# One change at four places of a two-layer hybrid encoder kernel: who shifts, who copies, and how the memory keys are loaded

## The chip, the cores and the metric

The kernel runs on one core of a Trainium2 chip. The metric is the device time of one execution in microseconds; lower is better. TensorE multiplies matrices, VectorE, ScalarE and GpSimd work on rows of 128 partitions, SyncE issues most of the DMA transfers.

## The reference, cut to what matters

```python
for i in range(DEPTH):                       # DEPTH = 2: dilated attention, then latent attention
    mix = dilated_mixer(...) if i % 2 == 0 else mla_mixer(...)
    kv = mem @ w_kv[i]                       # mem (256, 1024), w_kv (1024, 512): keys and values
    mo = memory_attention(qm, mem, w_kv[i])
    y = concat([mix, mo]) @ w_out
    x = layer_norm(ALPHA * x + y, ln_mix_g[i], ln_mix_b[i])
    f = hierarchical_moe(x, ...)             # 32 experts, top-2 inside the top-1 group
    x = layer_norm(ALPHA * x + f, ln_ffn_g[i], ln_ffn_b[i])
# layer_norm(x) = (x - mean) * rsqrt(var + eps) * g + b, over 1024 elements, for 1024 tokens
```

## The kernel before, in words

There are 1024 tokens in eight tiles of 128 (tile 0 to 7). Every engine runs its own list of instructions, written out by hand; semaphores tie them together.

**Head.** TensorE begins with `mem_projection(0)`: keys (16 products, contraction in eight slices of 128) into bank 6, then values (16 products) into bank 7. SyncE's `mem_loads` issues the transposed memory tokens (1 MB), the key half of the weights (1 MB) and the value half (1 MB). After them come the loads of the first of three head groups: query weights, the first half of x transposed, its second half, key and value weights. TensorE's `group_projection(0)` waits for query weights and the first half of x. ScalarE copies the keys out (`mem_keys`), VectorE the values. The same `mem_projection` and `mem_loads` come again for layer 1, at the end of the experts of layer 0.

**Layer norms.** There are four of them, i = 0 to 3: i = 0 and 2 in the output projections, i = 1 after the experts of layer 0, i = 3 after the experts of layer 1. For each tile VectorE adds up the tile (`combine`: L1910 and L1913 in layer 0, L1925 in layer 1), takes its statistics (L1675, L1678), ScalarE takes the root (L1355), VectorE computes 1/std (L1682) and -mean/std (L1683) in `tile_rstd`, one tile later in its order, and ScalarE normalises the tile (L1357). GpSimd's `norm_scale` multiplies the tile by g (L718) and adds b (L720), tiles 0 to 6; VectorE does both for tile 7 (`last_scale`, L1691 and L1693). In i = 1 the tile is then transposed by TensorE (L1000), copied by ScalarE (L1362) and VectorE (L1698), and projected. In i = 3 SyncE stores tile by tile, in order (`wait_tokens`, L685), and the kernel ends with the last store.

**Experts and overflow.** Each of the 32 experts takes up to 96 token rows. Rows above that go to overflow blocks, a loop after the experts whose count is read from memory. In this data it runs once, in layer 1. One round: TensorE transposes and multiplies, ScalarE applies silu (L1392), VectorE gates, TensorE multiplies by the down weights, VectorE copies the results out of the banks (four copies 32x256, L1836, and two copies 64x512, L1839), and GpSimd scatters them to DRAM (L803). In the ordinary expert loop ScalarE (L1407, L1408) and VectorE share these copies half and half. After the overflow SyncE loads all expert results (L656) and TensorE sums them with gates (`expert_sums`).

Lines shown as L825 are the helper of all ordinary products.

Of the kernel before, what the change touches and what calls it, by code (L numbers as in the profile page):

```python
# [22 lines left out]
ALU = mybir.AluOpType  # L23
# [3 lines left out]
P = 128  # L27
# [41 lines left out]
def build(nc, io):  # L69
    with ExitStack() as ctx:  # L70
# [56 lines left out]
        def ring_at(kb, *shape):  # L127
# [65 lines left out]
        mem_in = sem("mem_in")  # L193
        mem_v_in = sem("mem_value_weights_in")
# [53 lines left out]
        x_last = sem("x_last_ready")  # L248
        last_gmul = sem("last_gmul_done")
# [55 lines left out]
               ("w_in", "slots", "idx", "xs", "pe_steps", "silu", "dve_steps", "out")}  # L305
# [52 lines left out]

        def wait_tokens(eng, i, t):

            if t < TT - 1:
                eng.wait_ge(x_ready, i * (TT - 1) + t + 1)
            else:
                eng.wait_ge(x_last, i + 1)
# [94 lines left out]
        def _(sp):  # L459

            def mem_loads(l):
                w = io["mem_w_kv"][l].rearrange("(k p) n -> p k n", p=P)
                sp.dma_start(mem_t[l], io["mem_t"].rearrange("(k p) n -> p k n", p=P)).then_inc(mem_in, 16)
                sp.dma_start(mem_w[l][:, :, 0:GW], w[:, :, 0:GW]).then_inc(mem_in, 16)
# [225 lines left out]
        def _(pool):  # L690
# [20 lines left out]
            def norm_scale(i, store_to=None):  # L711

                pool.wait_ge(gb_in, 32 * (i + 1))
                for t in range(TT):
                    n = i * (TT - 1) + t + 1
                    if t < TT - 1:
                        pool.wait_ge(norm_done, i * TT + t + 1)
                        nc.gpsimd.tensor_tensor(X[:, t], X[:, t], ln_gb[:, 0], ALU.mult).then_inc(gmul_done, 1)  # L718
                        pool.wait_ge(gmul_done, n)
                        nc.gpsimd.tensor_tensor(X[:, t], X[:, t], ln_gb[:, 1], ALU.add).then_inc(x_ready, 1)  # L720
# [4 lines left out]
            def experts(l):  # L725
# [73 lines left out]
                with pool.If(n_over > 0):  # L799
                    with pool.Fori(0, n_over) as j:  # L800
                        pool.wait_ge(o["dve_steps"], 4 * j + 4)
                        fence(pool)
# [20 lines left out]
        def _(pe):  # L823
# [3 lines left out]
            def mem_projection(l):  # L827

                pe.wait_ge(mem_in, 32 * (l + 1))
                for j in range(2):  # L830
                    for k in range(KT):
                        mm(ps[:, 6, j * MEM:(j + 1) * MEM], mem_w[l][:, k, j * P:(j + 1) * P], mem_t[l][:, k], k == 0, k == KT - 1)
# [27 lines left out]
            def group_projection(g):  # L860
# [11 lines left out]
                pe.wait_ge(wv_in[b], 16 * uses)  # L872
                for t in range(9 if g == 0 else 8):
# [188 lines left out]
            def experts(l):  # L1062
# [57 lines left out]
                with pe.If(n_over > 0):  # L1120
                    with pe.Fori(0, n_over) as j:
# [9 lines left out]
                        pe.wait_ge(o["dve_steps"], 4 * j + 4)  # L1131
                        fence(pe)
# [152 lines left out]
        def _(act):  # L1285
# [10 lines left out]
            def mem_keys(l):  # L1296
                act.wait_ge(mem_proj, l + 1)
                nc.scalar.copy(km_t[:], ps[:, 6].rearrange("p (a b) -> p a b", a=2)).then_inc(mem_kv_act, 1)
# [95 lines left out]
            def experts(l):  # L1394
# [23 lines left out]
                o = ov[l]  # L1418
                act.wait_ge(over_done, l + 1)
                n_over = act.value_load(over_i[0:1, NOVER:NOVER + 1], min_val=0, max_val=NOVER)  # L1420
                with act.If(n_over > 0):
                    with act.Fori(0, n_over) as j:
                        act.wait_ge(o["pe_steps"], 4 * j + 2)
                        silu().then_inc(o["silu"], 1)
                with act.Else():
                    act.nop()
# [107 lines left out]
        def _(dve):  # L1534
# [145 lines left out]
            def tile_rstd(i, t):  # L1680
                dve.wait_ge(sd_done, i * TT + t + 1)
                ln_link(nc.vector.reciprocal(rstd[:, t, 0:1], std[:, t:t + 1]))  # L1682
                nc.vector.scalar_tensor_tensor(out=rstd[:, t, 1:2], in0=mean_var[:, t, 0:1], scalar=-1.0, in1=rstd[:, t, 0:1],  # L1683
# [452 lines left out]
```

## Time and profile before

| what | us |
|---|---|
| runs of the kernel | 2440.29, 2444.55, 2451.59 |
| their median | 2444.55 |
| profiled execution, its own time | 2438.25 |
| profiled execution, its span | 2436.1 |

| engine | busy us | share of the span |
|---|---|---|
| TensorE (matmul) | 2222.6 | 91% |
| VectorE | 841.7 | 35% |
| ScalarE | 468.2 | 19% |
| GpSimd | 343.0 | 14% |

The times in the rows below are microseconds from the start of the span, and durations; means of one instruction are in ns. PE is TensorE's matmul, PEld its weight load, DVE VectorE, ACT ScalarE, POOL GpSimd, SPq SyncE's queue. In a timeline row the bracket tells how long the engine sat idle before the instruction and which work released it. A granted clock of 1.00 is 2.4 GHz, 0.50 is 1.2 GHz.

### The profile page before, as it was taken

How to read it: one execution, taken by the hardware profiler on the slowest of the kernel's cores; microseconds unless marked ns; L12 is line 12 of the kernel's file. 1: busy time of each engine (PE TensorE's matmuls, PEld its weight loads, DVE VectorE, ACT ScalarE, POOL GpSimd, SP SyncE). 2: the span in 40 equal slices, each digit the busy share in tenths (PEclk: the TensorE clock that was granted, in tenths of full speed). 3: DMA queues.
4: the chain of work that ended last, by engine and by line, in shares of the span. 5: the costliest groups of instructions: out<-in, count | busy, mean ns of one | idle time of the engine just before them, and what ended most of it. 6: DMA issues, size and time to landing. Idle time of an engine off the chain costs nothing. (4 is left out here: it accounts for less than half of the span.)

```text
span 2436.1 us, 37961 instructions
## 1 busy us (share of the span) xinstructions
PE 2222.6 (91%) x15351; PEld 1184.0 (49%) x15351; DVE 841.7 (35%) x1791; ACT 468.2 (19%) x943; POOL 343.0 (14%) x401
## 2 busy tenths in 40 slices
PE   8999998886999999998797999989689999999964
PEld 4665757553444444444443556665444444444422
DVE  2133324634121212122825767642422212121216
ACT  0030304221010101011333444431201101010011
POOL 0000000141111111131600000003211111111305
PEclk9999998987999999999897999999689999999997
DMA  9022104344999999997310000010469999999945
GB/s 352 1 76 98 40 1 142 141 184 165 396 391 388 394 386 389 389 387 274 119 52 7 3 5 1 1 70 35 200 224 395 388 400 384 386 378 391 375 158 207
DMA packets 98871, 534.47 MB, mean 219 GB/s; under 512 B 23040, under 2 KB 46880, under 8 KB 73824
## 3 DMA queue, kind: packets, MB, share of 16 engines
q1 hardware_dynamic: 80672, 491.28, 51.8%
q0 software_dynamic: 18112, 41.99, 4.8%
q8 instruction: 60, 0.98, 0.2%
q14 instruction: 27, 0.22, 0.0%
HBM read 510.16 MB, written 41.45 MB: 226 GB/s over the span
## 5 line engine op out<-in xcount | busy, mean ns | idle before, releaser
L825 PE MATMUL banks<-ring,arena 128*32 128x256 f32 (+3 forms) x9952 | 1303.4, 461 | 38.5 <-DMA ring<-in_exp_w_gu 15.0
L825 PEld LDWEIGHTS banks<-ring,arena 128*32 128x32 f32 (+2 forms) x9952 | 536.4, 124 | 746.3 <-issue 608.7
L825 PE MATMUL banks<-ring 128*128 128x512 f32 (+2 forms) x976 | 372.2, 531 | 10.7 <-ACT ring L1468 7.1
L825 PEld LDWEIGHTS banks<-ring 128*128 128x128 f32 (+1 forms) x976 | 183.9, 194 | 156.6 <-issue 139.8
L1830 DVE TENSOR_TENSOR arena<-arena,banks 128x384 f32<-128x384 f32 x65 | 36.0, 554 | 609.7 <-ACT arena L1392 609.7
L761 POOL DMA_INDIRECT expert_out<-arena,scatter_idx x64 | 61.1, 955 | 824.4 <-DVE arena L1839 804.4
L1392 ACT ACTIVATE arena<-banks 128x384 f32<-128x384 f32 x65 | 31.9, 490 | 735.8 <-PE banks L825 735.8
L825 PE MATMUL banks<-arena 128*64 128x128 f32 (+5 forms) x1664 | 157.8, 303 | 16.7 <-DMA arena<-in_mem_w_kv 9.6
L825 PEld LDWEIGHTS banks<-arena 128*64 128x64 f32 (+3 forms) x1664 | 139.0, 169 | 50.2 <-issue 38.0
L718 POOL TENSOR_TENSOR arena<-arena,ln_gb 128x1024 f32<-128x1024 f32 x28 | 69.5, 2482 | 626.5 <-ACT arena L1357 626.5
L1836 DVE COPY arena<-banks 32x256 f32<-32x256 f32 x132 | 56.2, 425 | 280.1 <-PE banks L825 279.2
L825 PE MATMUL banks<-arena,ring 128*128 128x256 f32 (+3 forms) x288 | 101.0, 529 | 13.6 <-DVE ring L1977 11.7
L1407 ACT COPY arena<-banks 32x256 f32<-32x256 f32 x128 | 46.2, 361 | 313.7 <-PE banks L825 313.0
L1600 DVE CUSTOM_DVE_ANT_0 arena<-banks,arena 128x256 f32<-128x256 f32 (+1 forms) x160 | 54.1, 394 | 148.8 <-PE banks L825 145.5
L1989 DVE TENSOR_REDUCE max_and_sum<-banks 128x1 f32<-128x1024 f32 x64 | 77.5, 1212 | 38.6 <-PE banks L825 38.2
L1482 ACT ACTIVATE arena<-banks,neg_max 128x1024 f32<-128x1024 f32 x64 | 71.3, 1114 | 91.7 <-DVE neg_max L1991 90.5
L1031 PEld LDWEIGHTS banks<-ident,arena 96*128 96x128 f32 x520 | 47.5, 146 | 66.3 <-issue 63.4
L1357 ACT ACTIVATE arena<-arena,ln_rstd 128x1024 f32<-128x1024 f32 x32 | 39.7, 1240 | 191.2 <-DVE ln_rstd L1683 191.2
L1031 PE MATMUL banks<-ident,arena 96*128 96x96 f32 x520 | 59.7, 260 | 16.6 <-issue 8.5
L825 PEld LDWEIGHTS banks<-arena,ring 128*128 128x128 f32 (+2 forms) x288 | 48.6, 183 | 51.7 <-issue 47.0
L720 POOL TENSOR_TENSOR arena<-arena,ln_gb 128x1024 f32<-128x1024 f32 x28 | 71.1, 2539 | 2.2
L1826 DVE COPY arena<-banks 128x768 f32<-128x768 f32 x65 | 62.3, 958 | 24.9 <-PE banks L1031 17.5
(176 smaller groups left out, 1575.7 us busy)
## 6 DMA issues: line engine op xcount, KB each, us to landing
ring<-in_exp_w_gu SPq DMA_DIRECT2D x130, 2048.0 KB, 17.2
ring<-in_exp_w_down SPq DMA_DIRECT2D x65, 2048.0 KB, 21.8
ring<-in_x_t SPq DMA_DIRECT2D x6, 2304.0 KB, 16.4
moe_in<-arena POOLq DMA_DIRECT2D x16, 512.0 KB, 3.0
arena<-expert_out SPq DMA_DIRECT2D x16, 512.0 KB, 4.3
ring<-expert_out SPq DMA_DIRECT2D x16, 512.0 KB, 4.4
ring<-in_a_w_in SPq DMA_DIRECT2D x6, 1024.0 KB, 17.3
arena<-in_a_w_in SPq DMA_DIRECT2D x4, 1024.0 KB, 14.0
```

The lines of the kernel that those rows point to most:

```text
L718: nc.gpsimd.tensor_tensor(X[:, t], X[:, t], ln_gb[:, 0], ALU.mult).then_inc(gmul_done, 1)
L720: nc.gpsimd.tensor_tensor(X[:, t], X[:, t], ln_gb[:, 1], ALU.add).then_inc(x_ready, 1)
L761: pool.indirect_dma_start(y_d[l][:, :], bass.IndirectOffsetOnAxis(ap=s_idx[0:CAP, b:b + 1], axis=0), ys[0:CAP, b], None, bounds_check=2 * ...
L825: return nc.tensor.matmul(out, lhsT, rhs, start=start, stop=stop)
L1031: last = nc.tensor.transpose(ps[:, k // 4, (k % 4) * CAP:(k % 4 + 1) * CAP], xs[0:CAP, b, k * P:(k + 1) * P], ident[0:CAP, 0:CAP])
L1357: nc.scalar.activation(X[:, t], X[:, t], ACT.Identity, bias=rstd[:, t, 1:2], scale=rstd[:, t, 0:1]).then_inc(norm_done, 1)
L1407: nc.scalar.copy(ys[WIDE:CAP, b, g * 256:(g + 1) * 256], ps[NARROW * g:NARROW * g + NARROW, 7, 0:256])
L1482: nc.scalar.activation(prob[:, hd], ps[:, 2 * hd:2 * hd + 2].rearrange("p a b -> p (a b)"), ACT.Exp, bias=neg_max[:, hd, 0:1], scale=SCALE ...
L1600: last = nc.vector.tensor_tensor_reduce(out=prob[:, b, h * 256:h * 256 + w], in0=ps[:, 2 * b + h % 2, (h // 2) * 256:(h // 2) * 256 + w], ...
L1826: return V.tensor_copy(xs_t[b].rearrange("p (a c) n -> p a (c n)", a=2), ps[:, 0:2, 0:4 * CAP])
L1836: return V.tensor_copy(ys[WIDE:CAP, b, g * 256:(g + 1) * 256], ps[NARROW * g:NARROW * g + NARROW, 7, 0:256])
L1989: V.tensor_reduce(stat[:, hd, 0, 0:1], ps[:, 2 * hd:2 * hd + 2].rearrange("p a b -> p (a b)"), AX.X, ALU.max).then_inc(row_max, 1)
```

## The change

1. `mem_loads` loads the tokens and the key weights in two halves of the contraction, each half with a semaphore of its own. `mem_projection` does the products of the first half when it is there, then those of the second; its two 128-column halves of the keys lie in banks 5 and 6. TensorE waits for ScalarE's copy of the keys before it writes the value products of a group, which use bank 5.
2. In the last layer norm (i = 3) VectorE adds b for tiles 1, 3 and 5; GpSimd keeps all scales and the adds of tiles 0, 2, 4 and 6.
3. In the overflow round ScalarE copies half of the results, as in the expert loop.
4. In `tile_rstd` -mean/std is computed by an operation with one tensor input and a scalar per partition, in place of two tensor inputs and one scalar.

```diff
         def wait_tokens(eng, i, t):
-            if t < TT - 1:
+            if i == 3 and t in SHIFT_ON_DVE:          # SHIFT_ON_DVE = (1, 3, 5)
+                eng.wait_ge(x_shifted, SHIFT_ON_DVE.index(t) + 1)
+            elif i == 3 and t < TT - 1:
+                eng.wait_ge(x_ready, i * (TT - 1) + t + 1 - sum(o < t for o in SHIFT_ON_DVE))
+            elif t < TT - 1:
                 eng.wait_ge(x_ready, i * (TT - 1) + t + 1)
...
             def mem_loads(l):
-                sp.dma_start(mem_t[l], io["mem_t"].rearrange("(k p) n -> p k n", p=P)).then_inc(mem_in, 16)
-                sp.dma_start(mem_w[l][:, :, 0:GW], w[:, :, 0:GW]).then_inc(mem_in, 16)
+                for ks, landed in ((slice(0, KT // 2), mem_in), (slice(KT // 2, KT), mem_rest_in)):
+                    sp.dma_start(mem_t[l][:, ks], io["mem_t"].rearrange("(k p) n -> p k n", p=P)[:, ks]).then_inc(landed, 16)
+                    sp.dma_start(mem_w[l][:, ks, 0:GW], w[:, ks, 0:GW]).then_inc(landed, 16)
...
             def norm_scale(i, store_to=None):
-                        pool.wait_ge(gmul_done, n)
-                        nc.gpsimd.tensor_tensor(X[:, t], X[:, t], ln_gb[:, 1], ALU.add).then_inc(x_ready, 1)
+                        if not (i == 3 and t in SHIFT_ON_DVE):
+                            pool.wait_ge(gmul_done, n)
+                            nc.gpsimd.tensor_tensor(X[:, t], X[:, t], ln_gb[:, 1], ALU.add).then_inc(x_ready, 1)
...
                     with pool.Fori(0, n_over) as j:
                         pool.wait_ge(o["dve_steps"], 4 * j + 4)
+                        pool.wait_ge(o["y_act"], j + 1)
...
             def mem_projection(l):
-                pe.wait_ge(mem_in, 32 * (l + 1))
-                for j in range(2):
-                    for k in range(KT):
-                        mm(ps[:, 6, j * MEM:(j + 1) * MEM], mem_w[l][:, k, j * P:(j + 1) * P], mem_t[l][:, k], k == 0, k == KT - 1)
+                for half, landed in enumerate((mem_in, mem_rest_in)):
+                    pe.wait_ge(landed, 32 * (l + 1))
+                    for j in range(2):
+                        for k in range(4 * half, 4 * half + 4):
+                            mm(ps[:, 5 + j, 0:MEM], mem_w[l][:, k, j * P:(j + 1) * P], mem_t[l][:, k], k == 0, k == KT - 1)
...
             def group_projection(g):
                 pe.wait_ge(wv_in[b], 16 * uses)
+                pe.wait_ge(mem_kv_act, 1)
...
                         pe.wait_ge(o["dve_steps"], 4 * j + 4)
+                        pe.wait_ge(o["y_act"], j + 1)
...
             def mem_keys(l):
-                nc.scalar.copy(km_t[:], ps[:, 6].rearrange("p (a b) -> p a b", a=2)).then_inc(mem_kv_act, 1)
+                nc.scalar.copy(km_t[:], ps[:, 5:7, 0:MEM]).then_inc(mem_kv_act, 1)
...
                 o = ov[l]                                  # ScalarE, after its last expert
+                for b in range(2):
+                    act.wait_ge(ys_out[b], 16 * 16 * (l + 1))
...
                         silu().then_inc(o["silu"], 1)
+                        act.wait_ge(o["pe_steps"], 4 * j + 4)
+                        for g in range(2):
+                            nc.scalar.copy(ys[WIDE:CAP, 0, g * 256:(g + 1) * 256], ps[NARROW * g:NARROW * g + NARROW, 7, 0:256])
+                        nc.scalar.copy(ys[0:WIDE, 0, 0:HALF], ps[0:WIDE, 6]).then_inc(o["y_act"], 1)
...
             def tile_rstd(i, t):
-                nc.vector.scalar_tensor_tensor(out=rstd[:, t, 1:2], in0=mean_var[:, t, 0:1], scalar=-1.0, in1=rstd[:, t, 0:1],
-                                               op0=ALU.mult, op1=ALU.mult).then_inc(rs_done, 1)
+                nc.vector.tensor_scalar(rstd[:, t, 1:2], mean_var[:, t, 0:1], rstd[:, t, 0:1], -1.0, ALU.mult, ALU.mult).then_inc(rs_done, 1)
...
                         dve.wait_ge(o["pe_steps"], 4 * j + 4)
-                        for g in range(4):
+                        for g in range(2, 4):
                             narrow_out(0, g)
-                        wide_out(0, 0)
                         wide_out(0, 1).then_inc(o["dve_steps"], 1)
...
                     if t == TT:
                         last_scale(i)
+                    if l == 1 and t - 3 in SHIFT_ON_DVE:
+                        dve.wait_ge(gmul_done, i * (TT - 1) + t - 2)
+                        nc.vector.tensor_tensor(X[:, t - 3], X[:, t - 3], ln_gb[:, 1], ALU.add).then_inc(x_shifted, 1)
```

## Rows read from the trace of the kernel before

**Rows 1.** Stretches: start:end, length, PE, PEld, DVE, ACT, POOL, clock, DMA, GB/s.
```profile
600.00:1150.00 550.00, 538.69 (x4823) 240.70 (x4816) 109.84 (x188) 56.80 (x127) 85.14 (x134) 1.00 0.96 380
1777.00:1794.00 17.00, 15.40 (x116) 6.74 (x115) 10.55 (x21) 0.49 (x1) 2.58 (x5) 0.79 0.17 41
```
**Rows 2.** SyncE's timeline at the start; DMA issues with KB and us to landing.
```profile
0.74 0.44 SPq L463 DMA_DIRECT2D arena<-in_mem_t  x1
...
6.62 2.92 SPq L480 DMA_DIRECT2D ring<-in_x_t  x1
...
arena<-in_mem_t SPq DMA_DIRECT2D x1, 1024.0 KB, 5.7
...
ring<-in_x_t SPq DMA_DIRECT2D x1, 2304.0 KB, 14.9
```
**Rows 3.** TensorE's timeline: memory products of layer 0, and the gap in layer 1.
```profile
9.59 15.46 PE L825 MATMUL banks<-arena 128*128 128x256 f32 x64 [9.59 <-DMA arena<-in_mem_w_kv]
24.89 86.18 PE L825 MATMUL banks<-ring 128*128 128x512 f32 x272
...
1166.68 1.94 PE L1000 MATMUL banks<-ident,arena 128*128 128x128 f32 x8 [15.19 <-issue]
```
**Rows 4.** Timeline of one tile of the layer norm between the layers.
```profile
1182.87 3.22 POOL L720 TENSOR_TENSOR arena<-arena,ln_gb 128x1024 f32<-128x1024 f32 x1
...
1185.50 0.61 DVE L1683 SCALAR_TENSOR_TENSOR ln_rstd<-ln_mean_var,ln_rstd 128x1 f32<-128x1 f32 x1
...
1187.29 0.56 ACT L1362 COPY arena<-banks 128x512 f32<-128x512 f32 x1
...
1187.95 1.07 PE L1000 MATMUL banks<-ident,arena 128*128 128x128 f32 x8 [0.54 <-issue]
...
1195.28 1.06 PE L1000 MATMUL banks<-ident,arena 128*128 128x128 f32 x8 [0.68 <-issue]
```
**Rows 5.** Timeline: copies of the overflow round, and ScalarE's in an ordinary expert.
```profile
2367.47 1.72 DVE L1836 COPY arena<-banks 32x256 f32<-32x256 f32 x4 [5.62 <-PE banks L825]
2369.21 1.39 DVE L1839 COPY arena<-banks 64x512 f32<-64x512 f32 x2
...
1827.44 0.73 ACT L1407 COPY arena<-banks 32x256 f32<-32x256 f32 x2 [4.80 <-PE banks L825]
```
**Rows 6.** Timeline of the last layer norm, VectorE and GpSimd.
```profile
2392.29 0.16 DVE L1683 SCALAR_TENSOR_TENSOR ln_rstd<-ln_mean_var,ln_rstd 128x1 f32<-128x1 f32 x1
...
2392.88 1.22 DVE L1925 TENSOR_TENSOR arena<-arena,banks 128x1024 f32<-128x1024 f32 x1 [0.43 <-PE banks L825]
...
2396.31 1.22 DVE L1925 TENSOR_TENSOR arena<-arena,banks 128x1024 f32<-128x1024 f32 x1
...
2398.63 2.36 POOL L718 TENSOR_TENSOR arena<-arena,ln_gb 128x1024 f32<-128x1024 f32 x1
...
2399.02 0.11 DVE L1682 RECIPROCAL ln_rstd<-ln_std 128x1 f32<-128x1 f32 x1
...
2399.16 1.84 DVE L1683 SCALAR_TENSOR_TENSOR ln_rstd<-ln_mean_var,ln_rstd 128x1 f32<-128x1 f32 x1
...
2424.73 3.20 POOL L720 TENSOR_TENSOR arena<-arena,ln_gb 128x1024 f32<-128x1024 f32 x1
2425.77 3.24 DVE L1693 TENSOR_TENSOR arena<-arena,ln_gb 128x1024 f32<-128x1024 f32 x1
```
**Rows 7.** The last store, issued at 2429.04: us to landing; and a stretch (columns of rows 1).
```profile
DMA to landing us min/median/max: 2.8/2.8/2.8
...
2429.00:2430.00 1.00, 0.00 (x0) 0.00 (x0) 0.01 (x1) 0.00 (x0) 0.00 (x0) 0.50 1.01 406
```
**Rows 8.** Timeline in the routing of layer 0: GpSimd's memset, and VectorE's operations beside it.
```profile
547.21 1.80 POOL L728 MEMSET arena<- 128x2048 f32 x1 [9.71 <-PE banks L825]
...
548.53 0.19 DVE L1745 TENSOR_TENSOR arena<-logits,arena 128x32 f32<-128x32 f32 x1
548.64 0.41 DVE L1747 TENSOR_SCALAR arena<-arena 128x32 f32<-128x32 f32 x1
```

More of the change, by code:

```diff
@@ L193, in build @@
         mem_in = sem("mem_in")
+        mem_rest_in = sem("mem_rest_in")
         mem_v_in = sem("mem_value_weights_in")
@@ L248, in build @@
         x_last = sem("x_last_ready")
+        x_shifted = sem("x_shifted_by_dve")
         last_gmul = sem("last_gmul_done")
@@ L304, in build @@
         ov = [{n: sem(f"ov{l}_{n}") for n in
-               ("w_in", "slots", "idx", "xs", "pe_steps", "silu", "dve_steps", "out")}
+               ("w_in", "slots", "idx", "xs", "pe_steps", "silu", "dve_steps", "y_act", "out")}
               for l in range(DEPTH)]
@@ L357, in straight @@
                     step((0, u), u + 1 < TT, 0 <= u < TT, u >= 1)
+        SHIFT_ON_DVE = (1, 3, 5)
         def wait_tokens(eng, i, t):
-            if t < TT - 1:
+            if i == 3 and t in SHIFT_ON_DVE:
[3 more added lines that the diff above has]
+            elif t < TT - 1:
                 eng.wait_ge(x_ready, i * (TT - 1) + t + 1)
```

## Prediction

> **What bounds the kernel now.** I read the busy shares by stage first, then the timeline at each of the four places that the diff touches, since an average says nothing of a few microseconds. In the expert phases TensorE is busy 98% of the time at a granted clock of 1.00 [rows 1], and none of the four places lies in them: each is a stage with a limit of its own.
>
> *The head.* SyncE issues the memory tokens, the key weights behind them and, later, the first x. Tokens and x land at 0.74 + 5.7 = 6.4 and 6.62 + 14.9 = 21.5 us [rows 2]. TensorE starts its 32 memory products at 9.59, released by the key weights, and goes over to the group projection at 24.89 with no gap [rows 3]. So the first wait is a load and the next 15.3 us are TensorE's own.
>
> *The layer norm between the layers.* [Rows 4] show one token tile; the next one's transposes come 7.33 us later. The tiny L1683 (one element per partition) takes 0.61 us and ends just after GpSimd's L720 (1182.87 + 3.22 = 1186.09). ScalarE's norm waits for it, ScalarE's copy L1362 comes behind the norm, and TensorE's next transposes start when that copy is done (1187.95), after an idle 0.54 us.
>
> *The overflow block.* It runs once, in layer 1. VectorE copies four narrow and two wide results alone, 1.72 + 1.39 us from 2367.47 to 2370.60 [rows 5], and scatter, reloads and expert sums queue behind it.
>
> *The tail.* [Rows 6]: undisturbed L1683 takes 0.16 us; here it takes 1.84 and ends with GpSimd's op (2398.63 + 2.36 = 2400.99). Seven tiles times scale and shift keep GpSimd full, 14 ops of some 2.35 us. The last one is stretched to 3.20 us by VectorE's scale of tile 7, and VectorE's shift (L1693) waits in turn until 2427.93 and ends at 2429.01. Two-tensor operations of the two engines exclude each other. The stage is one chain through that shared access.
>
> **The change, part by part.**
>
> *Keys in halves.* The first half of tokens and of key weights is as many bytes as the tokens alone, so it lands near 6.4 instead of 9.4 us; two more issues at about 0.44 us each [rows 2] stand ahead of loads that wait for bandwidth, so I cost them at 0.1 us of the start. TensorE begins at about 6.5. Half of the key products takes some 5 us (15.46 us for 32, the first ones slower), to 11.5, when the second half has landed: it is there when the whole was, 9.5. No new wait. All end at 24.89 - 3.1 = 21.8, and the first x landed at 21.5: covered by 0.3 us. **3.0 us**; with x landing 0.5 us late it is 2.7. The bounds are 0 (TensorE waits for x or for the second half) and 3.1. The added wait for the key copy stands ahead of the value products, 50 us after that copy: nothing. Group projections and attention follow TensorE, and the loads behind them are triggered by it, so the gain is carried on. In layer 1 the same split gains nothing: TensorE idles 15.19 us behind the memory products there [rows 3], waiting for the first normalised tile. The five issues there stand ahead of one load only.
>
> *The small operation*, between the layers. If it no longer waits, L1683 takes the 0.16 us of its undisturbed form [rows 6], ScalarE's copy comes 0.45 us earlier, and TensorE's gap of 0.54 us shrinks by that. VectorE asks for the shared access for the next tile's sum 0.4 us earlier, just as it comes free at 1186.09, so the tile's cycle shrinks from 7.33 to about 6.9 us; TensorE's own work is 7.33 - 0.68 = 6.65. Five tiles have such a gap (two of them in rows 4): 5 x 0.4 = **2.0 us**. Bounds 0 and 5 x 0.54 = 2.7. In the two output projections the operation already takes 0.16 us in the median: 0.
>
> *Overflow copies.* VectorE keeps two of four narrow copies and one of two wide ones, 0.86 + 0.70 = 1.56 us in place of 3.13. ScalarE's half runs beside it, as in every expert, where its two narrow copies take 0.73 us [rows 5] and its wide one is of VectorE's order. The function table that ScalarE loaded ahead of the tail is now loaded after these copies, 1.28 us, ended 15 us before its first use. ScalarE, GpSimd and TensorE wait for semaphores that are set by then. **1.5 us**, bounds 1.2 and 1.6.
>
> *Three shifts on VectorE*, with a small operation that does not wait. TensorE hands over a tile every 3.43 us (2392.88, 2396.31 [rows 6]) and VectorE's work on one is 3.0 us (2392.88 to 2395.88). From GpSimd's scale of tile 1, which ends at 2401.0: scale 2 to 2403.4; VectorE shift 1, asked for at 2399.75 + 3.0 = 2402.8, to 2404.5 (1.08 us each, the part of L1693 after 2427.93); GpSimd shift 2 to 2406.8, scale 3 to 2409.2, scale 4 to 2411.6; VectorE's tile 6 work ends at 2410.7 and shift 3 runs to 2412.7; GpSimd shift 4 to 2415.0, scale 5 to 2417.4, scale 6 to 2419.9; VectorE scale 7 to 2421.0, GpSimd shift 6 to 2423.3, VectorE shift 7 to 2424.4. Only then, since the code puts it behind the scale and shift of tile 7, shift 5 to 2425.5. What comes late is the store: SyncE waits in order of tiles, so tiles 5, 6 and 7 are issued together from 2425.5. Now the last store lands 2.8 us after 2429.04, at 2431.8; the last two are 1.05 MB at 406 GB/s [rows 7], 2.6 us, so 1.3 us of latency from the issue at 2427.95. Three are 3.9 us, after the same latency from 2425.5: 2430.7. So of 3.5 us on the engines the end sees **1.2 us**; bounds -2.9 (below) and 3.5.
>
> **Sum:** 3.0 + 2.0 + 1.5 + 1.2 = 7.7 us. The profiled execution took 2438.25 us for a span of 2436.1, so 2430.5; the median of the runs shown is 6.3 us above it, and the forecast for the median is 2444.55 - 7.7 = **2436.9 us**.
>
> **The rivals.**
>
> *The small operation still waits.* [Rows 8] show a VectorE operation with one tensor input, 128x32, of 0.41 us that ends just when GpSimd's memset ends (547.21 + 1.80 = 549.01); tensor operations of two inputs beside it took 0.19 us and did not wait. So one input is no safe pass. Then the 2.0 us between the layers are gone. In the tail tile 2's norm comes at 2401.0 as before, scale 2 ends at 2404.8, shift 1 at 2405.9, and on: shift 2 2408.2, scale 3 2410.6, scale 4 2414.3, shift 3 2415.4, shift 4 2417.8, scale 5 2420.2, scale 6 2423.9, shift 6 2426.3, VectorE 2427.4, 2428.5 and shift 5 2429.6; stores land at 2429.6 + 1.3 + 3.9 = 2434.8, 3 us later than now. Sum 3.0 + 1.5 - 2.9 = 1.6 us: 2442.9. For it: the 0.41 us. Against: the reciprocal beside L1683, of one element and one input, takes 0.11 us with GpSimd running [rows 6].
> [...]
>
> *The clock* (the slower side). The first expert of layer 1 ran in a stretch with a mean granted clock of 0.79, most of the expert phase at 1.00 [rows 1], where an expert takes about 550 / 32 = 17 us. If work shifted by 3 us leaves the clock at 1.2 GHz for one more expert, its 17 us become 34: 2436.9 + 17 = 2453.9, slower than before. It decides from a low stretch that costs 7.7 us, 15.4 us long at half speed. Nothing in the diff asks for it; the runs shown, 11.3 us apart, show that such amounts occur. The same in our favour gives about 2428.
>
> *The head's gain does not come*, because the first x lands later behind more issues, or the halves land together: 7.7 - 3.0, 2439.9.
>
> **How the numbers follow.** Forecast 0.52, small operation still waiting 0.26, head without gain 0.08, clock against 0.06, clock in favour 0.08. The range is 2429 to 2446: it takes in the first three cases with their bounds and some microseconds of scatter, and leaves out the clock cases. A measurement of this kernel can tell about 0.5%, 12.2 us, from no change. 7.7 us is 0.3%: faster by more takes the clock's help, 0.12; slower by more two mishaps, 0.03; within it 0.85.
>
> **What would show it.** TensorE's first product near 6.5 us and the group projection near 21.9. L1683's successor at 0.16 us everywhere; 0.6 and 1.8 us would be the first rival. TensorE's gaps in the norm between the layers below 0.3 us. Overflow copies over in 1.6 us. GpSimd with 11 operations in the tail, over 4.6 us sooner (2423.3 for 2427.9, the gains before it aside), three stores issued together. Wrong would be: a gap ahead of the group projection, shifts of tiles 1 and 3 that hold up the next tile's sum by more than a microsecond, or a time outside 2429 to 2446.

## The result, and the profile after

| | before | after |
|---|---|---|
| median of 8 runs, us | 2441.34 (2440.00 to 2451.59) | 2428.40 (2424.64 to 2433.50) |
| profiled execution, its own time | 2438.25 | 2429.48 |
| its span | 2436.1 | 2427.6 |
| ratio of the runs, with its 95% interval | | 0.9946 [0.9933, 0.9959] |

The change is 0.54% faster, 12.9 us in the medians and 8.5 us in the two spans. The forecast was 2436.9 us, a gain of 7.7. Of the 8.5 us between it and the measured 2428.4, 3.2 are the reference's (three runs of before had a median of 2444.55, eight have 2441.34) and 5.2 are a gain larger than forecast.

In the rows below the line numbers are those of the changed kernel: TensorE's helper is L836, its transposes L1013, the small operation L1703, GpSimd's scale L727 and add L730, VectorE's scale and add of tile 7 L1710 and L1712, its new adds L1957, the last store L694.

**The head.** TensorE's timeline (start, duration, engine, line, operation, count, and in the bracket the idle time and its releaser); it answers to [rows 3]:

```profile
6.80 15.63 PE L836 MATMUL banks<-arena 128*128 128x256 f32 x64 [6.80 <-DMA arena<-in_mem_w_kv]
22.26 8.32 PE L836 MATMUL banks<-ring 128*128 128x512 f32 x19
```

TensorE starts 2.79 us earlier and reaches the group projection 2.63 us earlier (22.26 for 24.89), with no gap in the products and none ahead of the projection. Neither the second half nor the first x is waited for; x lands at 6.77 + 14.9 = 21.7, 0.6 us ahead of the projection.

**Between the layers.** All eight uses of the small operation in this stage, before and then after (duration in ns: min/median/max), and two tiles' transposes after; they answer to [rows 4]:

```profile
L1683 DVE SCALAR_TENSOR_TENSOR ln_rstd<-ln_mean_var,ln_rstd x8: 159/600/607, 1158.2 to 1204.0; 128x1 f32<-128x1 f32 x8
```
```profile
L1703 DVE TENSOR_SCALAR ln_rstd<-ln_mean_var,ln_rstd x8: 214/214/215, 1156.9 to 1201.0; 128x1 f32<-128x1 f32 x8
```
```profile
1185.27 2.65 POOL L727 TENSOR_TENSOR arena<-arena,ln_gb 128x1024 f32<-128x1024 f32 x1 [0.98 <-ACT arena L1371]
...
1185.77 1.06 PE L1013 MATMUL banks<-ident,arena 128*128 128x128 f32 x8 [0.28 <-issue]
...
1192.70 1.06 PE L1013 MATMUL banks<-ident,arena 128*128 128x128 f32 x8 [0.28 <-issue]
...
1207.01 1.06 PE L1013 MATMUL banks<-ident,arena 128*128 128x128 f32 x8 [0.73 <-DVE arena L1717]
```

The operation takes 0.214 us every time, whether GpSimd runs beside it or not. TensorE's gap is 0.28 us where it was 0.54 and 0.68, and a tile takes 6.93 us (1192.70 - 1185.77) where it took 7.33. GpSimd now starves: it waits 0.98 us for ScalarE's norm. The last gap of this stage stays: ahead of one tile's transposes TensorE waits 0.73 us for VectorE's copy, as it did in the kernel before:

```profile
1209.98 1.06 PE L1000 MATMUL banks<-ident,arena 128*128 128x128 f32 x8 [0.73 <-DVE arena L1698]
```

**Overflow.** Timeline of the copies, which answers to [rows 5]:

```profile
2365.23 0.73 ACT L1443 COPY arena<-banks 32x256 f32<-32x256 f32 x2 [7.40 <-PE banks L836]
2365.23 0.86 DVE L1855 COPY arena<-banks 32x256 f32<-32x256 f32 x2 [5.62 <-PE banks L836]
2365.97 0.58 ACT L1444 COPY arena<-banks 64x512 f32<-64x512 f32 x1
2366.11 0.69 DVE L1858 COPY arena<-banks 64x512 f32<-64x512 f32 x1
2366.57 1.28 ACT L1369 ACT_TABLE_LOAD   x1
```

VectorE is done in 1.57 us (2365.23 to 2366.80) instead of 3.13, ScalarE beside it in 1.32. The table load stands where it was expected and nobody waits for it.

**The tail.** VectorE's first add of a tile's sums, before and then after, and after from the first of the new adds on; the last answers to [rows 6, 7]:

```profile
2386.08 1.22 DVE L1925 TENSOR_TENSOR arena<-arena,banks 128x1024 f32<-128x1024 f32 x1 [15.49 <-PE banks L825]
```
```profile
2383.10 1.22 DVE L1943 TENSOR_TENSOR arena<-arena,banks 128x1024 f32<-128x1024 f32 x1 [16.30 <-PE banks L836]
...
2399.74 1.72 DVE L1957 TENSOR_TENSOR arena<-arena,ln_gb 128x1024 f32<-128x1024 f32 x1
...
2407.32 2.08 DVE L1957 TENSOR_TENSOR arena<-arena,ln_gb 128x1024 f32<-128x1024 f32 x1
...
2415.65 1.63 DVE L1710 TENSOR_TENSOR arena<-arena,ln_gb 128x1024 f32<-128x1024 f32 x1 [1.38 <-ACT arena L1371]
2416.28 3.20 POOL L730 TENSOR_TENSOR arena<-arena,ln_gb 128x1024 f32<-128x1024 f32 x1
2417.32 3.25 DVE L1712 TENSOR_TENSOR arena<-arena,ln_gb 128x1024 f32<-128x1024 f32 x1
2420.49 1.21 DVE L1957 TENSOR_TENSOR arena<-arena,ln_gb 128x1024 f32<-128x1024 f32 x1
2421.73 1.64 SPq L694 DMA_DIRECT2D out_x<-arena  x3
```

The three stores go out together, as foreseen. To compare executions I count from VectorE's first add of tile sums, 2386.08 before and 2383.10 after, to the end of the span, and call this **the tail**: 50.0 us before, 44.5 after. The tail term was forecast at 1.2 us and is 5.5.

Most of the expectations below count from the first product of the expert sums instead, 2379.92 before and 2376.43 after: 56.2 and 51.2 us. That count takes in TensorE's sums for the first tile, and these depend on the granted clock: in the first 15 us of the expert sums it was 0.84 before, 0.81 after and 0.88 in a second trace of the changed kernel (y1), and VectorE's first add came 6.2, 6.7 and 5.6 us after the first product. From the first add on, executions of one kernel agree within 0.03 us.

Where the rest is, the last rows tell. First SyncE's waits at its end (total us, count, longest), before and then after; behind them, before, the traffic after the last store was issued (columns of rows 1):

```profile
SPq L70 <- PEq L70: 4.0, 1, 4.0
SPq L70 <- DMA out_x<-arena: 2.5, 1, 2.5
```
```profile
SPq L70 <- DMA out_x<-arena: 3.6, 1, 3.6
SPq L70 <- PEq L70: 0.5, 1, 0.5
```
```profile
2431.00:2432.00 1.00, 0.00 (x0) 0.00 (x0) 0.00 (x0) 0.00 (x0) 0.00 (x0) 0.50 0.36 139
...
2433.00:2436.00 3.00, 0.00 (x0) 0.00 (x0) 0.00 (x0) 0.00 (x0) 0.00 (x0) 0.50 0.00 0
```

Before, the last store had landed at 2429.04 + 2.8 = 2431.8 and the span still ran for 4.3 us, in which nothing moves and no engine is busy. SyncE sits those 4.0 us at the program's last line, behind the wait for its stores. After, the wait for the stores is longer (three at once) and the one behind it is 0.5 us. The name PEq is no help: TensorE had long been done. GpSimd's last operation is its add, which ends at 2424.73 + 3.20 = 2427.93 before and at 2419.48 after, and the span ends 8.2 us behind it in both (8.16 by the unrounded trace).

What lies between is recorded. At the program's last line each engine has an instruction DRAIN. GpSimd's and SyncE's before, then GpSimd's after (view of L70: duration in ns, start):

```profile
L70 POOLq DRAIN  x1: 11172/11172/11172, 2424.7 to 2424.7; - x1
...
L70 SPq DRAIN  x1: 13/13/13, 2432.0 to 2432.0; - x1
```
```profile
L70 POOLq DRAIN  x1: 11176/11176/11176, 2416.2 to 2416.2; - x1
```

GpSimd's ends at 2424.7 + 11.2 = 2435.9 before, 7.9 us after its add and 3.8 us after SyncE's; then the engines exchange semaphores and the span ends 0.2 us later. The description ahead of the prediction, by which the kernel ends with the last store, is not borne out. Why GpSimd's DRAIN takes 7.9 us beyond its last operation, no run here shows.

### The profile page after: what moved, and what is told of

It is laid out like the page before. It is cut to its first block and busy times, and to the rows that moved or that the text cites. A ratio compares the mean times of both kernels' runs of the same rounds, so it can differ in the third digit from the quotient of the medians.

```text
span 2427.6 us, 37971 instructions
## 1 busy us (share of the span) xinstructions
PE 2220.2 (91%) x15351; PEld 1185.3 (49%) x15351; DVE 833.2 (34%) x1791; ACT 469.4 (19%) x946; POOL 338.9 (14%) x398
## 5 line engine op out<-in xcount | busy, mean ns | idle before, releaser
L836 PE MATMUL banks<-ring,arena 128*32 128x256 f32 (+3 forms) x9952 | 1302.0, 461 | 38.5 <-DMA ring<-in_exp_w_gu 16.1
L836 PEld LDWEIGHTS banks<-ring,arena 128*32 128x32 f32 (+2 forms) x9952 | 536.6, 124 | 744.6 <-issue 606.8
L836 PE MATMUL banks<-ring 128*128 128x512 f32 (+2 forms) x976 | 369.3, 528 | 11.9 <-ACT ring L1488 7.1
L836 PEld LDWEIGHTS banks<-ring 128*128 128x128 f32 (+1 forms) x976 | 182.4, 192 | 156.9 <-issue 140.4
L836 PE MATMUL banks<-arena 128*64 128x128 f32 (+5 forms) x1664 | 159.0, 305 | 14.0 <-DMA arena<-in_mem_w_kv 6.8
L836 PEld LDWEIGHTS banks<-arena 128*64 128x64 f32 (+3 forms) x1664 | 140.1, 170 | 47.2 <-issue 34.9
L727 POOL TENSOR_TENSOR arena<-arena,ln_gb 128x1024 f32<-128x1024 f32 x28 | 69.4, 2481 | 627.0 <-ACT arena L1371 627.0
L836 PE MATMUL banks<-arena,ring 128*128 128x256 f32 (+3 forms) x288 | 99.4, 523 | 13.8 <-DVE ring L1998 11.7
L836 PEld LDWEIGHTS banks<-arena,ring 128*128 128x128 f32 (+2 forms) x288 | 48.4, 182 | 50.6 <-issue 45.7
L758 POOL DMA_INDIRECT arena<-moe_in,gather_idx x64 | 62.9, 983 | 55.5 <-POOL gather_idx L755 55.5
```

Of the source, the lines that this page charges most:

```text
L758: pool.indirect_dma_start(xs[0:CAP, b], None, x1_d[l][:, :], bass.IndirectOffsetOnAxis(ap=g_idx[0:CAP, b:b + 1], axis=0), bounds_check=S - ...
L836: return nc.tensor.matmul(out, lhsT, rhs, start=start, stop=stop)
```

## The experiments

Two theories of the tail: the span ends with the last store's landing (as the prediction had it), or it ends some 8.2 us after GpSimd's last operation, unless the stores land later. And for each part of the change: what is it worth alone, and with the others? All times of the table are from one profiled execution each. The second column counts from the first product of the expert sums to the end of the span; the tail, the end of GpSimd's last operation and the issue and landing of the last store count from VectorE's first add.

| kernel | from the first product | tail | GpSimd's end | last store issued | last store landed | ratio of the runs |
|---|---|---|---|---|---|---|
| before | 56.2 | 50.0 | 41.9 | 43.0 | 45.8 | |
| the change | 51.2 | 44.5 | 36.4 | 39.5 | 43.9 | 0.9946 [0.9933, 0.9959] |
| the change again (x0) | 51.1 | 44.5 | 36.4 | 39.5 | 43.9 | 0.9945 [0.9928, 0.9963] |
| the change again (y1) | 50.1 | 44.5 | 36.4 | 39.5 | 43.9 | 0.9953 [0.9936, 0.9970] |
| small operation alone (x1) | 57.6 | 51.0 | 42.9 | 43.3 | 46.9 | 0.9992 [0.9978, 1.0005] |
| shifts alone (x2) | 55.4 | 48.9 | 39.8 | 44.2 | 48.5 | 1.0001 [0.9988, 1.0013] |
| overflow copies alone (x3) | 55.2 | 50.0 | 41.9 | 43.0 | 45.8 | 1.0002 [0.9991, 1.0013] |
| halves alone (x4) | 56.0 | 50.0 | 41.9 | 43.0 | 45.8 | 1.0003 [0.9991, 1.0016] |
| halves alone, again (x11) | 56.2 | 50.0 | 41.9 | 43.0 | 45.8 | 0.9998 [0.9987, 1.0010] |
| before, GpSimd touched last (x5) | 57.7 | 51.3 | 43.1 | 43.0 | 45.8 | 1.0014 [0.9999, 1.0029] |
| change with the two-input operation (x7) | 55.7 | 48.9 | 39.8 | 44.2 | 48.6 | 0.9983 [0.9972, 0.9993] |
| change, tile 6 shifted too (x6) | 47.8 | 42.2 | 33.1 | 38.1 | 41.9 | 0.9936 [0.9914, 0.9957] |
| the same again (y3) | 49.1 | 42.3 | 33.1 | 38.1 | 41.9 | 0.9951 [0.9934, 0.9968] |
| change, shifts placed earlier (x9) | 50.1 | 44.5 | 36.4 | 38.8 | 41.4 | 0.9966 [0.9953, 0.9978] |
| tile 6 too, and earlier (x8) | 48.6 | 42.1 | 33.1 | 38.1 | 41.7 | 0.9946 [0.9929, 0.9964] |
| change without halves (x10) | 51.3 | 44.5 | 36.4 | 39.5 | 43.9 | 0.9964 [0.9951, 0.9976] |
| the same again (y2) | 51.2 | 44.5 | 36.4 | 39.5 | 43.9 | 0.9952 [0.9934, 0.9970] |

**The change again (x0), no edit.**

> The changed kernel once more, for a second trace of it and of its scatter. If the clock's steps are what moved TensorE by up to 4 us between stages, they fall in other places here, while the tail (from VectorE's first tile sum to the end of the span) takes the same 44.5 us, within 0.2. If the tail varies by more, part of the tail's gain is scatter too.

From VectorE's first tile sum to the end 44.5 us, as expected; group projection at 22.1, the small operation 0.214 us in the median: all repeated.

**GpSimd touched last (x5).** GpSimd waits for VectorE's last add and then sets 128 words that nobody reads:

```diff
+            pool.wait_ge(x_last, 4)
+            nc.gpsimd.memset(eps[:, 1:2], RMS_EPS).then_inc(zeroed, 1)
```

> The kernel before with one more GpSimd operation, a memset of one element per partition that waits for tile 7 to be finished (at 2429.0 in the trace of before), beside the last store. Theory D counted from the start of GpSimd's last operation: the span ends 11.2 us after 2429.1, 4.3 us later than before. Theory D counted from its end (7.9 us): the memset takes 0.1 us, so the span ends near 2437.1, 1.2 us later. Theory S (4.3 us after the last store lands): unchanged, within 0.3 us.

The timeline's last lines, SyncE's waits and GpSimd's DRAIN of this kernel:

```profile
2428.16 1.41 SPq L685 DMA_DIRECT2D out_x<-arena  x2
2429.28 0.10 POOL L821 MEMSET eps<- 128x1 f32 x1 [1.14 <-DVE arena L1695]
```
```profile
SPq L70 <- PEq L70: 5.2, 1, 5.2
SPq L70 <- DMA out_x<-arena: 2.5, 1, 2.5
```
```profile
L70 POOLq DRAIN  x1: 8052/8052/8052, 2429.3 to 2429.3; - x1
```

Stores as before, and an operation of 0.10 us on GpSimd, ended at 2429.38, moves the end to 2437.5, 8.2 us behind it; GpSimd's DRAIN ends at 2437.3, again 7.9 us behind the operation. SyncE's last wait grows from 4.0 to 5.2 us, by as much as GpSimd's end moved from its add (2424.93 + 3.20 = 2428.13, now 2429.38: 1.25). The end is tied to GpSimd. The table says the same of all: wherever the last store is issued at most 3.1 us after GpSimd's end, tail minus GpSimd's end is 8.2 us (8.16 or 8.17 before rounding; before, the change and its repeats, x1, x3, x4, x5, x9, x10, x11, y2), whether the last landing is 0.7 or 5.5 us ahead of the end. Where the stores are later (x2, x6, x7, x8, y3) it is 9.0 to 9.2, and the tail ends 0.4 us behind the last landing (0.39 or 0.40 before rounding); in x6 SyncE's DRAIN is at 2422.8, GpSimd's is over at 2411.4 + 10.5 = 2421.9. So in all 17 executions the span ends with the later of two, GpSimd's last operation plus 8.2 us and the last landing plus 0.4.

**The shifts alone (x2).** Of the change's diff only `SHIFT_ON_DVE`, the waits in `wait_tokens`, the skipped add in `norm_scale` and the add in `combine`.

> The kernel before with the three shifts on VectorE alone; the small operation keeps its two tensor inputs. Theory D (the span ends when GpSimd's queue drains, 11.2 us after its last operation starts, or with the last store if that is later): VectorE's waits for GpSimd stay, so GpSimd's last operation starts only some 0.6 us earlier and the stores land 2.6 us later, which brings both ends together: the span is 0 to 1 us shorter. Theory S (the span ends 4.3 us after the last store lands, as my prediction had it): 2.6 us longer. Both within 0.2%, so the trace decides: which comes last, and by how much.

Two of GpSimd's operations in its timeline:

```profile
2402.84 2.35 POOL L725 TENSOR_TENSOR arena<-arena,ln_gb 128x1024 f32<-128x1024 f32 x1
...
2406.56 2.35 POOL L725 TENSOR_TENSOR arena<-arena,ln_gb 128x1024 f32<-128x1024 f32 x1 [1.37 <-ACT arena L1365]
```

GpSimd has three operations of 2.35 us less, 7 us, and its end moves by 2.1: it now sits idle for ScalarE's norm, 4.3 us in all, since the norm waits for VectorE's small operation and that for GpSimd. The last store lands 2.7 us later than before, yet the tail is 1.1 us shorter: the end didn't follow the stores here either. The gain of 1.1 us isn't seen in the runs.

**The small operation alone (x1).**

```diff
-                nc.vector.scalar_tensor_tensor(out=rstd[:, t, 1:2], in0=mean_var[:, t, 0:1], scalar=-1.0, in1=rstd[:, t, 0:1],
-                                               op0=ALU.mult, op1=ALU.mult).then_inc(rs_done, 1)
+                nc.vector.tensor_scalar(rstd[:, t, 1:2], mean_var[:, t, 0:1], rstd[:, t, 0:1], -1.0, ALU.mult, ALU.mult).then_inc(rs_done, 1)
```

> The kernel before with the small operation alone. Between the layers TensorE's gaps shrink to 0.28 us: 1.6 us gained, as in the trace of the changed kernel. In the tail GpSimd still has 14 operations and nothing is taken off it. Theory D: its last operation starts no earlier, perhaps 1 us later, because VectorE no longer keeps out of step with it: sum -1.6 to 0 us. Rival (the small operation alone gives the tail's gain): -1.6 - 4 = -5.6 us.

From the first transposes of this stage (TensorE's L1000) to the first product behind the last ones 49.1 us (1171.26 to 1220.36) instead of 50.7 (1166.68 to 1217.35): 1.6 gained between the layers. In the tail 1.0 lost: VectorE is done early with tile 7, GpSimd has all 14 operations and is the last, as its rows show:

```profile
2420.15 3.32 POOL L718 TENSOR_TENSOR arena<-arena,ln_gb 128x1024 f32<-128x1024 f32 x1
2423.55 3.20 POOL L720 TENSOR_TENSOR arena<-arena,ln_gb 128x1024 f32<-128x1024 f32 x1
2426.72 2.33 POOL L718 TENSOR_TENSOR arena<-arena,ln_gb 128x1024 f32<-128x1024 f32 x1
2429.13 2.34 POOL L720 TENSOR_TENSOR arena<-arena,ln_gb 128x1024 f32<-128x1024 f32 x1
```

**The change with the old small operation (x7).** The reverse of the diff above, in the changed kernel.

> The changed kernel with the small operation undone (two tensor inputs again). Between the layers the gaps of TensorE go back from 0.28 to 0.54 to 0.7 us: 1.6 us lost. In the tail VectorE waits for GpSimd in every tile again. Theory D: GpSimd's last operation starts about 4 us later than in the changed kernel, stores land 4 us later: together 5.5 to 6 us slower than the changed kernel, 2.5 to 3.5 us faster than before. Rival: the small operation has little part in it, and the tail's gain comes from the shifts alone: 1.6 us slower than the changed kernel.

Tail 48.9 us, as with the shifts alone, and 50.7 us between the layers. VectorE's small operation, up to 2.02 us in the tail, is what binds the two engines to each other. So in the tail the shifts alone give 1.1 us, the small operation alone costs 1.0, and both give 5.5: the two are one measure. Against the change the old operation costs 4.4 + 1.6 = 6.0 us in the traces and 6.25 in the medians (2436.15 to 2429.9 of the change beside it), a little more than expected, and the rival's 1.6 is excluded.

**Tile 6 shifted too (x6, y3), and the order of the adds (x9, x8).**

```diff
-        SHIFT_ON_DVE = (1, 3, 5)
+        SHIFT_ON_DVE = (1, 3, 5, 6)
```

> The changed kernel with VectorE adding b for tile 6 as well, so GpSimd's last operation is the scale of tile 6. Theory D: GpSimd's last operation starts 2.4 us earlier and ends 3.4 us earlier, the stores land nearly 5 us earlier, and the span is shorter than that of the changed kernel by 2.4 us (counted from the start) or 3.2 us (from the end). Theory S: shorter by 4.9 us. Against the kernel before: a ratio of about 0.993 to 0.9945.

```profile
2409.26 4.64 POOL L727 TENSOR_TENSOR arena<-arena,ln_gb 128x1024 f32<-128x1024 f32 x2
...
2413.34 1.64 DVE L1710 TENSOR_TENSOR arena<-arena,ln_gb 128x1024 f32<-128x1024 f32 x1 [1.38 <-ACT arena L1371]
2415.01 1.23 DVE L1712 TENSOR_TENSOR arena<-arena,ln_gb 128x1024 f32<-128x1024 f32 x1
2416.16 2.36 DVE L1957 TENSOR_TENSOR arena<-arena,ln_gb 128x1024 f32<-128x1024 f32 x2
```

GpSimd ends at 2413.9, VectorE's add of tile 7 takes 1.23 us instead of 3.25 with GpSimd out of the way, and the tail is 42.2 us: 2.3 shorter (by the count of the expectation 47.8, 3.4 shorter, but 1.1 of that is the clock in the first tile's sums). Now the stores end last, 4.1 us after the last issue at 2418.92. The next two runs move VectorE's adds ahead of tile 7's, without and with tile 6:

```diff
-                    if t == TT:
-                        last_scale(i)
                     if l == 1 and t - 3 in SHIFT_ON_DVE:
                         dve.wait_ge(gmul_done, i * (TT - 1) + t - 2)
                         nc.vector.tensor_tensor(X[:, t - 3], X[:, t - 3], ln_gb[:, 1], ALU.add).then_inc(x_shifted, 1)
+                    if t == TT:
+                        last_scale(i)
```

> The change with one thing altered: VectorE's shift of tile 5 stands ahead of the scale and shift of tile 7. Theory that GpSimd's last operation sets the end: it still has the add of tile 6 last, at the same time, so the tail stays at 51.2 us (50.7 to 51.7) although the stores are issued earlier; median as the change, within 1 us. Rival, that the stores set the end, as the prediction had it: tile 5 stored 2.3 us earlier, tail 49 us.

> The change with VectorE adding b for tiles 1, 3, 5 and 6 too, and with the shift of a tile placed ahead of the scale and shift of tile 7 in VectorE's order, so that tile 5 is stored earlier. Theory that the span ends with the later of two, GpSimd's last operation plus 7.9 us and the last store's landing: with shift 6 on VectorE alone the end was the stores' (last issue at 2418.92, tail of 47.8 us from the first expert sum). Moved ahead, shift 5 lets its store go some 2.3 us earlier, so the three last stores no longer queue: tail 46.5 us (46.0 to 47.2), GpSimd's last operation as there, and a median about 1.3 us below that of shift 6 alone. Rival, that the order costs as much as it gives because the scale of tile 7 comes later: tail 47.8 or more.

x9: the last store lands 2.5 us earlier (41.4 for 43.9), GpSimd's end is unmoved (36.4), and so is the tail (44.5). That is the expectation, seen once the count starts at VectorE's first add; from the first product the tail reads 50.1, because the granted clock in the first 15 us of the sums was 0.88 and not 0.81. SyncE's waits say the same (2.3 us for the stores, then 2.9):

```profile
SPq L70 <- PEq L70: 2.9, 1, 2.9
SPq L70 <- DMA out_x<-arena: 2.3, 1, 2.3
```

The runs of x9 were no faster than the change's (2432.26), and y1, the change unaltered, has the same 50.1 at the same clock. x8 has a tail of 42.1, only 0.15 us less than x6 and y3: the rival was right, tile 7 pays for the earlier tile 5.

**Overflow copies alone (x3).** The hunks of `y_act` and ScalarE's three copies.

> The kernel before with the overflow copies shared alone. From the end of the down products to the scatter's issue 1.5 us less, and nothing else moves: -1.5 us in the span, 0.06%, below what the timing can tell; the trace has to show it. Rival: ScalarE's table load or the added wait holds up the tail: 0.

From the gating to the scatter 9.9 us (2359.57 to 2369.47) instead of 11.4 (2360.10 to 2371.47): 1.5 gained in the trace. The runs don't resolve it.

**The halves alone (x4, x11), and the change without them (x10, y2).** The hunks of `mem_loads`, `mem_projection`, `mem_keys` and the wait in `group_projection`, added to the kernel before, and taken from the changed one.

> The kernel before with the memory keys in halves alone. TensorE starts at 6.8 us and the group projection at 22.3: -2.6 us. Theory carried on: the whole of it is left at the start of the layer norm between the layers, and the span is 2.6 us shorter, plus or minus the clock's steps of up to 4 us seen between the two traces. Rival: the later stages give it back, because the experts are bound by loads that do not start earlier: 1.2 to 1.4 us left after the experts of layer 0, as in the trace of the changed kernel.

> The halves alone, once more, beside the other kernels of this call. In the trace the gain of 3.2 us was there at the start of layer 1's experts and gone in the span, where TensorE had spent 107 us at the lower clock in the latent attention stage instead of 85 to 99. Theory that this is scatter of the clock: starts at group projection 22.4, ratio 0.9987 (0.9980 to 1.0000). Rival, that the halves alone put the kernel into a worse course of the clock each time: ratio 1.000 to 1.002 and over 100 us at the lower clock in that stage again.

> The change without the halves of the memory loads; the other three parts stay. If the head's gain of 3.2 us is carried through the whole kernel: group projection at 25.7 instead of 22.3, span and median 3.2 us longer than the change, ratio to before about 0.9960. Rival, that the gain is lost on the way (the halves alone gave no difference in the timed rounds, 1.0003 [0.9991, 1.0016]): ratio as the change, 0.9946 to 0.995.

TensorE's timeline at the start, of x4 and of x10:

```profile
6.41 16.14 PE L827 MATMUL banks<-arena 128*128 128x256 f32 x64 [6.41 <-DMA arena<-in_mem_w_kv]
22.39 3.17 PE L827 MATMUL banks<-ring 128*128 128x512 f32 x7
```
```profile
9.58 17.04 PE L834 MATMUL banks<-arena 128*128 128x256 f32 x64 [9.58 <-DMA arena<-in_mem_w_kv]
26.46 1.88 PE L834 MATMUL banks<-ring 128*128 128x512 f32 x4
```

The traces are clear for the first half of the kernel. Over the nine executions with halves (x8 left out: its first attention took some 9 us longer, at a mean granted clock of 0.94 where the change had 0.97) and the seven without, the mean start of the group projection is 22.3 against 25.7 us, of the first expert's transposes 569.7 against 573.2, and of the first transposes between the layers 1164.8 against 1168.5, the last difference uncertain by about 1.6 us. Further on they don't show it. The expert sums start at 2377.1 against 2380.2, but the kernels with halves have the overflow copies and the new small operation more often than those without, which accounts for 0.9 of these 3.1 us; the 2.2 that are left are uncertain by about 3. The runs see less. Halves alone: 1.0003 with an interval from 0.9991, which leaves out 3 us (0.9988), and 0.9998 with one from 0.9987, which just takes it in; together a mean of 2441.0 us in 23 runs, where the kernel before beside them has 2441.2 in 46. Of the two readings of x11 the rival, a worse course of the clock each time, fell: from its first product to the experts' first transposes the latent attention took 551.7 us in x4, the longest of all, and 543.0 in x11, the shortest. Three kernels were then timed side by side:

> The change itself again, beside the two kernels of this call. Ratio to before 0.9945 (0.993 to 0.996), tail 51.1 us from the first expert sum to the end of the span.

> The change without the halves of the memory loads, again, in one call with the change. Theory that the head's gain reaches the end: the median is 3 us (1.5 to 4.5) above the change's of this call, as it was across calls (0.9964 to 0.9946). Rival, that the gain is lost in the stages behind, as the two runs of the halves alone suggest (1.0003 and 0.9998): within 1 us of the change's.

> The change with VectorE adding b for tile 6 too (in the change's own order), again, in one call with the change. Theory that the end follows GpSimd's last operation until the stores take over: tail 47.8 us, 3.3 us shorter than the change, median 3 us (1.5 to 4.5) below it. Rival, that the profile's end is not what the time sees: within 1 us of the change's.

Medians 2428.75, 2429.59 and 2429.32. The change's ratio came as expected (0.9953), its count from the first product did not (50.1 for 51.1, the clock in the first tile's sums). Both other medians lie within 1 us of the change's, where their rivals had them, but six to nine runs that spread over 7 to 15 us exclude neither side. Over all runs, the mean is 2429.4 for the change (23 runs), 2430.3 without halves (12) and 2426.8 with tile 6 shifted too (12), each uncertain by about 1.5 to 3 us. The halves' 3 us are in the traces up to the layer norm between the layers; in the time they are not shown, and the runs of the halves alone speak against the whole of them. The best kernel measured is x6/y3, by about 2.6 us in the mean, not certain beyond its scatter.

**What scatters.** The latent attention is the same code in all these kernels. The same stretch before and in x7 (start:end, length, PE, PEld, DVE, ACT, POOL, clock, DMA, GB/s):

```profile
1219.00:1784.00 565.00, 504.00 (x2780) 303.94 (x2780) 302.90 (x616) 197.76 (x359) 44.13 (x31) 0.90 0.11 42
```
```profile
1219.00:1780.00 561.00, 496.99 (x2781) 301.58 (x2781) 303.36 (x617) 197.82 (x359) 44.16 (x31) 0.92 0.11 43
```

The same products take 504 us at a mean granted clock of 0.90 and 497 at 0.92. Over all executions that stage, from its first product (1228.52 before) to the first transposes of layer 1's experts (1775.84), ranges from 543.0 to 551.7 us. A gain of 3 us upstream is smaller than that.

## Why the prediction was right, and where it failed

**What failed is one step, the tail's last sentence**: "So of 3.5 us on the engines the end sees 1.2 us"; the term measured 5.5. It took the landing of the last store for the end. Its own figures show the gap: the store lands at 2431.8, the span ends at 2436.1, and 4.3 us were left unexplained. They belong to GpSimd: the program isn't over until 8.2 us after GpSimd's last operation (x5, and eleven more rows of the table). With that, the step's own arithmetic gives GpSimd 4.6 us sooner (2423.3 for 2427.9, which the text lists among the signs and doesn't count), and a tail of 50.0 - 4.6 = 45.4; measured 44.5.

The schedule itself held within 0.9 us. Counted from VectorE's first add of tile sums (2386.08 before, 2383.10 after):

| | predicted | measured |
|---|---|---|
| VectorE's add of tile 1 ends | 18.4 | 18.4 |
| VectorE's add of tile 3 ends | 26.6 | 26.3 |
| GpSimd's last operation ends | 37.2 | 36.4 |
| VectorE's add of tile 7 ends | 38.3 | 37.5 |
| VectorE's add of tile 5 ends | 39.4 | 38.6 |
| last store lands | 44.6 | 43.9 (3.6 us after its issue ended at 2423.37) |

The stores' gain was 1.9 us for 1.2: landing at 45.8 before and 43.9 after. One sign that the prediction had named as wrong did come: VectorE's shifts hold up its next tile sum, that of tile 5 by 1.2 us and that of tile 7 by 2.3 (18.3 and 26.2 us after the first add, for 17.1 and 24.0 in x1, which has no shifts). It cost the tail next to nothing, since GpSimd's 11 operations still ran with only 0.1 us of idle time between them.

**The other terms.** The head: forecast 3.0, 2.6 in the profiled pair, 3.3 over the 16 executions; its cover (x landing 0.3 us ahead) held. That the gain is carried on to the end is not shown. Between the layers: 2.0 forecast, 1.6 measured (50.7 to 49.1 in every kernel with the new operation). The prediction counted five gaps that shrink; the trace before has four (0.54, 0.68, 0.67 and 0.73 us), and the last stays, because TensorE waits for VectorE's copy there; and the operation takes 0.21 and not 0.16 us. Overflow: 1.5 and 1.5 (scatter after gating 11.37, now 9.89). Sum with the tail's 5.5: 3.3 + 1.6 + 1.5 + 5.5 = 11.9 us, against 12.9, 11.7 and 11.4 in the medians of three sets of runs. In the profiled pair the terms make 2.6 + 1.6 + 1.5 + 5.5 = 11.2, and the spans differ by 8.5: 1.2 us of the head's lead are gone at the first transposes between the layers (1166.68 before, 1165.27 after), 0.5 go in the first tile's sums, and the other 1.0 between them.

**The rivals.** *The small operation still waits*: fell, 0.214 us in all places. The Trainium skill's rule (SBUF — State Buffer, "Who interferes with whom", with the condition of VectorE: DVE Perf Modes, "Mode 2×_2P") has a VectorE operation with one tensor input contend with GpSimd only in a mode that needs an outermost non-unit dimension that is even, or odd and equal in source and destination. One element per partition has no non-unit dimension, so by the rule the new operation doesn't contend, and the trace agrees with its 0.214 us. The rival's computed order of events is that of x7, though, where the old operation stays: last store landed 48.7 us after the first add by the rival (2434.8 - 2386.1), 48.6 in x7. *The clock*: its price was right in kind, as the latent attention's 543 to 552 us show, but in the profiled pair that stage took 547.3 us in both. *The head's gain doesn't come*: it came in every trace at the group projection; whether the time has it is open.

**The range** was short by 0.6 us at its lower end for two reasons of like size, the tail (4.3 us) and the three runs' median (3.2). Each alone would have stayed inside. The second is luck of the three runs and no mechanism. The chance for "faster" by over 0.5%, 0.12, followed from the same step: with the tail at 5.5 us the sum would have been 12.0, next to the 12.2 us that make 0.5%.

## What to carry to other kernels

Before the end of a kernel is priced, account for the whole stretch from the last transfer's landing to the end of the span: if microseconds are left over, look which engine's last operation stands a fixed time ahead of the end in another execution too. Here that was GpSimd, so its last operation, and not the last store, was to be made early. Count a stage from a point behind the stretch that the clock moves: from the first product, repeats of one kernel differed by 1.1 us, from VectorE's first add by 0.01. And of two edits to one coupled stage, price the pair: here one was worth 1.1 us alone, the other -1.0, and both together 5.5.

## What the hardware showed

- The program's end lay 8.2 us after the end of GpSimd's last operation in twelve of the seventeen executions, even if that operation was a 0.10 us memset (x5). In the other five it lay 0.4 us after the last store's landing. GpSimd's DRAIN at the program's last line ended 7.9 us after its last operation in all seventeen.
- An operation on one element per partition with one tensor input never waited for GpSimd (0.212 to 0.216 us), while the same with two inputs took from 0.16 to 2.02 us.
- With GpSimd idle a VectorE add of 128x1024 takes 1.2 us, with GpSimd's running beside it 3.25: in x6, where GpSimd is done by then, VectorE's add of tile 7 is 2 us shorter (1.23 us).
- The course of TensorE's clock in unchanged code moved its stage by up to 8.7 us from one execution to the next, more than the head, the small operation between the layers and the overflow copies were worth together (6.4).
